# Differential attention's scores: one fp32 product or three fp32r products of split queries and keys

## The chip, the cores and the metric

The kernel runs on one core of one Trainium2 chip. The metric is the time of one execution on the device in microseconds. Three runs of the kernel before gave 3485.47, 3486.98 and 3488.18 us, median 3486.98.

## What is computed

Two stacks of two layers each run over 1024 tokens of width 1024, all in float32. The first stack mixes convolutions, a windowed attention and a neighbourhood attention. The second one has, per layer, a chunkwise retention, a differential attention, an output product and a gated feed-forward part. The change is in the differential attention of the second stack:

```
def diff_attention(q, k, v, lam):        # q, k: (B, S, 4 heads, 2 maps, 64)   v: (B, S, 4, 128)
    for i in range(S // 128):            # 8 blocks of 128 queries
        q0, kend = 128 * i, 128 * (i + 1)
        s = einsum('bqhjd,bkhjd->bhjqk', q[:, q0:kend], k[:, :kend]) * d ** -0.5
        s = s - slopes * dist            # ALiBi
        s = where(dist >= 0, s, -inf)    # causal
        p = softmax(s)
        a = p[:, :, 0] - lam * p[:, :, 1]
        outs.append(einsum('bhqk,bkhe->bqhe', a, v[:, :kend]))
```

Each head has two maps (j = 0, 1) whose softmaxes are subtracted, so a block of queries has 4 heads x 2 maps of scores against all keys up to its own block.

## The kernel before, in words

Everything is kept transposed: a chunk is 128 channels on the partitions by 1024 tokens. `st` is a store of 23 such slots in SBUF. Dense products are done to fp32 accuracy with three fp32r matmuls: every operand is split into a rounded part (`hi`) and the rest (`lo`), and hi·hi, hi·lo and lo·hi are summed in PSUM. A dense product (line 784) of 128 output channels uses two PSUM banks (0 and 1, or 2 and 3), is evacuated by VectorE (DVE), and counts in the semaphores `done` (TensorE) and `taken` (DVE). GpSimd (POOL) splits the weights for the next products (lines 619 and 622, in the values' stage 646 and 649) when `done` frees their buffer.

The differential attention of a layer is a list of 40 steps on each of three engines, written out by hand. Unit u = 4n + t is head t of query block n (n from 0 to 7), 32 units in all. The keys of a block are up to 8 tiles of 128; blocks 0 to 3 are one piece of 128, 256, 384 or 512 columns, blocks 4 to 7 are two pieces (384 and 256, 384 and 384, 512 and 384, 512 and 512). For a piece there is a pair of scores, one for each map: map j lies on the partitions 64j to 64j + 63 of the head's slot (queries in slots 4 to 7, keys in 18 to 21), so the two matmuls of a pair use different rows of the array, and write banks 4 and 5.

Step u of **TensorE** does in this order: turn the first group of tiles of unit u - 3 (line 926, bank 6); the scores of unit u's first piece (line 876); in some steps turn back a block's heads (line 960); weigh the values with unit u - 4 (line 943, bank 7); turn the second group; the scores of the second piece. Between the steps it does the matmuls of five dense products of the output projection (26 to 30), spread by the cuts (0, 7, 14, 20, 34, 40): a `product` first waits for `taken` of the one before.

Step u of **VectorE**: the mix of the two maps of unit u - 2 (lines 1842, 1843, 1847); the bias and running minimum of the first piece, once for each map (line 1825, `CUSTOM_DVE_ANT_0`, then a short read of its accumulator), which reads banks 4 and 5 and signals `biased`; the same for the second piece; and in steps with u % 4 of 0 and 1 the root and the factor of a block's heads (lines 1740 to 1745, 1853, 1860, 1874). At each cut it adds a dense product to x (line 1683).

Step u of **ScalarE** (ACT): it copies the turned groups out of bank 6 (line 1320), does the two exponentials of unit u - 1 (line 1306), and in steps with u % 4 of 3 copies the weighed block out of bank 7 and squares it (lines 1331, 1335); at the end of a block it writes the turned-back heads into slots 4 to 7 (line 1346).

The order of a pair before: the matmul of map 0 waits for `biased` of the previous map 0, the one of map 1 for `biased` of the previous map 1.

Just ahead of the attention TensorE runs the last value product (line 818) and the dense products 24 and 25. ScalarE issues the load of the bias table after value product 22; VectorE evacuates those values (line 1675), adds product 24 to x, waits for the table, adds product 25 to x and starts. Product 26 waits until product 24 has been added.

The two attentions of the first stack, windowed (`gqa`) and neighbourhood (`na`), already score with three fp32r products (line 897), with the parts made by `key_hi`, `query_hi` (ScalarE) and `key_lo`, `query_lo` (VectorE, lines 1784 to 1794).

## Time and profile before

| | |
|---|---|
| median of three runs | 3486.98 us (3485.47 to 3488.18) |
| the profiled execution | 3486.82 us, of which the span is 3484.7 us |
| TensorE busy | 3402.9 us, 98% |
| VectorE busy | 1954.8 us, 56% |
| ScalarE busy | 977.4 us, 28% |
| GpSimd busy | 1485.9 us, 43% |
| chain that ended last | TensorE 82%, issue 9%, VectorE 6%, GpSimd 2% |
| of it lines 784 and 1201 (dense products) | 44% and 23% |
| lines 943 and 926 (attention's values and turns) | 3% and 2% |
| old scores, line 876 | 384 records, 1392.0 to 2713.1 us |

The differential attentions lie at about 1392 to 1560 us and, in the second layer, at about 2580 to 2750 us. A busy TensorE isn't TensorE at its peak: matmuls overlap, and a record's duration holds its latency. In rows with "x4" four records follow each other closely and the duration is from the first start to the last end. A row's bracket gives the engine's idle time before it and what ended that. The granted clock (PEclk) is 1.00 at 2.4 GHz and 0.50 at 1.2 GHz.

### The profile page before, as it was taken

What the parts mean: (1) busy time and instruction counts of PE and PEld (TensorE: products, weight loads), DVE (VectorE), ACT (ScalarE), POOL (GpSimd) and SP (SyncE); (2) the same over time, 40 slices, a digit from 0 to 9 for tenths busy, and PEclk for the clock granted to TensorE, in tenths of its full rate; (3) what the DMA queues carried; (4) which work ended last, traced back from release to release, by engine and by line L of the source; (5) the groups of instructions that cost most, each with busy time, mean ns of one, the idle gap of its engine ahead of it and who ended that gap; (6) DMA issues with size and microseconds to landing.
All of it is one profiled execution on the core that took longest, in us unless ns stands there. A gap on an engine that the chain in (4) does not pass through costs nothing.

```text
span 3484.7 us, 43637 instructions
## 1 busy us (share of the span) xinstructions
PE 3402.9 (98%) x17144; PEld 2785.2 (80%) x17144; DVE 1954.8 (56%) x2937; ACT 977.4 (28%) x1831; POOL 1485.9 (43%) x952
## 2 busy tenths in 40 slices
PE   8999999999999999999999999999998999999997
PEld 7888788888788989567888888889885778888885
DVE  5777645777647143768656542332457775655315
ACT  2220442230342000655333320100035543333102
POOL 4435324435324433016555535643330365564543
PEclk9999999999999999999999999999999999999998
DMA  4112102102101111003222152111110122223411
GB/s 152 43 41 67 57 25 85 43 31 83 58 19 43 50 43 66 13 13 121 85 79 85 73 205 84 54 50 54 37 55 7 67 97 79 85 79 133 154 69 73
DMA packets 72821, 240.38 MB, mean 69 GB/s; under 512 B 21952, under 2 KB 22336, under 8 KB 66240
## 3 DMA queue, kind: packets, MB, share of 16 engines
q1 hardware_dynamic: 50112, 205.54, 16.6%
q10 hardware_dynamic: 22528, 32.31, 2.9%
q8 instruction: 127, 2.08, 0.2%
q14 instruction: 54, 0.44, 0.0%
HBM read 196.94 MB, written 41.68 MB: 68 GB/s over the span
## 4 chain that ended last, share of the span: by engine, by line
PE 82%; issue 9%; DVE 6%; POOL 2%; DMA 1%; ACT 1%; ACTq 0%; DVEq 0%; POOLq 0%
PE ps L784 44%; PE ps L1201 23%; PE ps L818 5%; PE ps L943 3%; PE ps L897 2%; PE ps L926 2%; POOL w_lo L622 1%; DVE st L1983 1%; POOL w_hi L619 1%; DVE st L1701 1%; DVE in_lo L1692 0%; DVE sl_r L2343 0%; PE ps L833 0%; PE ps L1121 0%; DVE xt L1683 0%
## 5 line engine op out<-in xcount | busy, mean ns | idle before, releaser
L619 POOL TENSOR_TENSOR w_hi<-w_raw,ones_r 128x512 fp32r<-128x512 f32 x316 | 406.5, 1286 | 1402.3 <-PE ps L784 1372.8
L1201 PE MATMUL ps<-sl_r,sl_r 128*128 128x512 f32 x3696 | 845.7, 391 | 5.1 <-DVE sl_r L2293 2.9
L1201 PEld LDWEIGHTS ps<-sl_r,sl_r 128*128 128x128 f32 x3696 | 696.1, 189 | 153.2 <-DVE sl_r L2293 3.8
L784 PE MATMUL ps<-in_hi,w_hi 128*128 128x512 f32 x1920 | 613.4, 401 | 14.8 <-DVE in_lo L1692 10.3
L784 PE MATMUL ps<-in_hi,w_lo 128*128 128x512 f32 x1920 | 600.8, 394 | 0.0
L784 PE MATMUL ps<-in_lo,w_hi 128*128 128x512 f32 x1920 | 598.9, 393 | 0.0
L622 POOL TENSOR_TENSOR w_lo<-w_raw,w_hi 128x512 fp32r<-128x512 f32 x316 | 465.4, 1473 | 24.8
L784 PEld LDWEIGHTS ps<-in_hi,w_hi 128*128 128x128 f32 x1920 | 348.4, 189 | 106.4 <-issue 38.7
L784 PEld LDWEIGHTS ps<-in_hi,w_lo 128*128 128x128 f32 x1920 | 358.4, 189 | 81.3 <-issue 5.7
L784 PEld LDWEIGHTS ps<-in_lo,w_hi 128*128 128x128 f32 x1920 | 359.7, 189 | 79.6 <-issue 4.4
L784 PE MATMUL ps<-sl_r,w_hi 128*128 128x512 f32 x1408 | 376.5, 389 | 0.2
L706 POOL TENSOR_TENSOR sl_r<-sl,sl_r 128x1024 fp32r<-128x1024 f32 x88 | 221.9, 2524 | 308.6 <-ACT sl_r L1557 303.4
L1683 DVE TENSOR_TENSOR xt<-xt,ps 128x1024 f32<-128x1024 f32 x112 | 136.7, 1220 | 351.4 <-PE ps L784 350.7
L2310 DVE TENSOR_TENSOR sl_r<-raw_pair,sl_r 128x1024 fp32r<-128x1024 f32 x84 | 196.9, 2383 | 216.5 <-ACT sl_r L1557 216.5
L784 PEld LDWEIGHTS ps<-sl_r,w_hi 128*128 128x128 f32 x1408 | 264.2, 188 | 55.9 <-DVE sl L2337 1.1
L1667 DVE TENSOR_TENSOR st<-ps,rfac 128x1024 f32<-128x1024 f32 x88 | 107.4, 1223 | 244.9 <-PE ps L784 227.0
L784 PE MATMUL ps<-sl_r,w_lo 128*128 128x512 f32 x704 | 216.7, 389 | 0.0
L1320 ACT ACTIVATE st<-ps 128x384 f32<-128x384 f32 (+3 forms) x256 | 122.9, 480 | 331.8 <-PE ps L926 331.3
L943 PEld LDWEIGHTS ps<-st 128*128 128x128 f32 x1504 | 184.3, 193 | 26.5 <-ACT st L1320 15.3
L1983 DVE SCALAR_TENSOR_TENSOR st<-st,cur 128x1023 f32<-128x1023 f32 (+14 forms) x128 | 199.5, 1559 | 2.0
L943 PE MATMUL ps<-st 128*128 128x64 f32 (+1 forms) x1504 | 198.0, 274 | 0.0
L1574 ACT ACTIVATE ps<-ps 128x512 f32<-128x512 f32 x132 | 76.8, 582 | 296.3 <-PE ps L1201 296.3
(218 smaller groups left out, 4249.2 us busy)
## 6 DMA issues: line engine op xcount, KB each, us to landing
w_raw<-w_in SPq DMA_DIRECT2D x184, 512.0 KB, 3.2
raw_pair<-w_ffn SPq DMA_DIRECT2D x44, 1024.0 KB, 4.8
hid_kept<-sl SPq DMA_DIRECT2D x44, 512.0 KB, 2.6
sl<-hid_kept SPq DMA_DIRECT2D x44, 512.0 KB, 8.5
x_put_away<-xt SPq DMA_DIRECT2D x16, 512.0 KB, 7.7
xt<-x_put_away SPq DMA_DIRECT2D x16, 512.0 KB, 6.2
xt<-x_in ACTq DMA_DIRECT2D x8, 512.0 KB, 8.0
space_lo<-c_alibi ACTq DMA_DIRECT2D x2, 2048.0 KB, 8.7
```

The lines of the kernel that those rows point to most:

```text
L619: pool.tensor_tensor(w_hi[:, j, cols], w_raw[:, j, cols], ones[:, 0:1].broadcast_to([P, HALF]), ALU.mult).then_inc(pool_own, 1)
L622: rest = pool.tensor_tensor(w_lo[:, j, cols], w_raw[:, j, cols], w_hi[:, j, cols].bitcast(F32), ALU.subtract)
L706: pool.tensor_tensor(sl_r[:, RING[p % 2][lo], :], pair_sums(p)[i], sl_r[:, RING[p % 2][hi], :].bitcast(F32), ALU.subtract).then_inc(pair_s ...
L784: last = pe.matmul(ps[:, 2 * j + h, :], w[:, w_slot, (w_k + k) * P:(w_k + k + 1) * P], part[:, k0 + k, h * HALF:(h + 1) * HALF], start=(k ...
L818: last = pe.matmul(out, x[:, k, tokens], w[:, 0:2, k * P:(k + 1) * P], start=(k == 0 and b % 2 == 0 and x is in_hi and w is w_hi), stop=(k ...
L943: last = pe.matmul(ps[:, 7, t * width:(t + 1) * width], turned_buffer(kind, g)[:, b * P:(b + 1) * P], value(t, kt), start=(kt == tiles[0]) ...
L1201: last = pe.matmul(ps[:, to[name], :], ring(sl_r, p, wp[w])[:, k * P:(k + 1) * P], half_of(sl_r, xp[x], k), start=(name in ("P1", "P5") an ...
L1320: act.activation(turned_buffer(kind, g)[:, 0:w], ps[:, 6, 0:w], ACT.Copy).then_inc(turned_out.handle, 1)
L1667: dve.tensor_tensor(to, ps[:, 2 * j:2 * j + 2, :].rearrange("p a b -> p (a b)"), rfac[:, :], ALU.mult).then_inc(taken.handle, 1)
L1683: last = dve.tensor_tensor(xt[:, c, :], xt[:, c, :], flat(ps, 2 * (n % 2), 2), ALU.add)
L1983: return dve.scalar_tensor_tensor(acc[:, a:b], source[:, a + d:b + d], weight, acc[:, a:b], ALU.mult, ALU.add)
L2310: dve.tensor_tensor(lo, source, hi.bitcast(F32), ALU.subtract).then_inc(pair_lo.handle, 1)
```

## The change

Queries and keys of the differential attention are split as in the other two attentions, and each score becomes three fp32r products. In detail:

- The four key slots (18 to 21) are copied, rounded, into slots 14, 16, 17 and 22 by ScalarE, and VectorE overwrites them with the rests. ScalarE does this after it has issued the table's load, VectorE after it has evacuated the values and before the first addition to x. The queries of blocks 0 and 1 follow on both.
- The rounded queries lie in a ring for two blocks in `rfac`; the rests overwrite the queries in slots 4 to 7. For blocks 2 to 7 ScalarE makes the rounded part at the end of step 4n - 3, VectorE the rest in step 4n - 2, after its second piece.
- `rfac` held the finished heads; these now share the buffer with the raw heads in slot 15. ScalarE's copy of raw heads waits for `back` in place of `headed` of two blocks earlier.
- TensorE waits for the query rest at a block's first unit. A pair of scores is six matmuls after one wait for `biased` of the previous pair's second map; each map's third product signals `scored`.

```
             if kind == "dif":                                  # head_buffer
-                return rfac[:, (n % 2) * HALF:(n % 2 + 1) * HALF]
+                return raw_buffer(n)

+        K_HI_DIF = (14, 16, 17, 22)
+            if kind == "dif":                                  # key_parts
+                return st[:, 18 + c, :], st_r[:, K_HI_DIF[c], :], st_r[:, 18 + c, :]
+            if kind == "dif":                                  # query_parts
+                block = slice(n * P, (n + 1) * P)
+                ring = rfac_r[:, :].rearrange("p (b t q) -> p b t q", b=2, t=4)
+                return st[:, 4:8, block], ring[:, n % 2], st_r[:, 4:8, block]

                     if kind == "dif":                          # TensorE, scores(u, i)
+                        if t == 0 and i == 0:
+                            pe.wait_ge(qk_lo.handle, qk_lo.at(stack, l, split_index(kind, n)))
+                        _, q_hi, q_lo = query_parts(kind, n)
+                        _, k_hi, k_lo = key_parts(kind, t)
                         for piece in pieces_of(tiles_of_round(kind, n))[i:i + 1]:
-                            for j in range(2):
-                                p, rows = state["p"], slice(HD * j, HD * (j + 1))
-                                if p >= 2:
-                                    pe.wait_ge(biased.handle, biased.at(stack, l, p0 + p - 1))
-                                pe.matmul(ps[:, 4 + j, 0:len(piece) * P], st[rows, 4 + t, n * P:(n + 1) * P],
-                                          st[rows, 18 + t, cols], start=True, stop=True).then_inc(scored.handle, 1)
-                                state["p"] += 1
+                            cols, p = slice(piece[0] * P, (piece[-1] + 1) * P), state["p"]
+                            if p >= 2:
+                                pe.wait_ge(biased.handle, biased.at(stack, l, p0 + p))
+                            for q, k in ((q_hi, k_hi), (q_lo, k_hi), (q_hi, k_lo)):
+                                for j in range(2):
+                                    rows = slice(HD * j, HD * (j + 1))
+                                    last = pe.matmul(ps[:, 4 + j, 0:len(piece) * P], q[rows, t, :], k[rows, cols],
+                                                     start=(q is q_hi and k is k_hi), stop=(k is k_lo))
+                                    if k is k_lo:
+                                        last.then_inc(scored.handle, 1)
+                            state["p"] += 2

-                        act.wait_ge(headed.handle, headed.at(stack, l, r0 + n - 1))
+                        act.wait_ge(back.handle, back.at(stack, l, r0 + n - 1))
-                    if kind != "dif" and u % 4 == 1 and 2 <= u // 4 + 1 < NB:
+                    if u % 4 == 1 and 2 <= u // 4 + 1 < NB:
                         query_hi(stack, l, kind, u // 4 + 1, p0)
+                for c in range(4):                             # ScalarE, ahead of the attention
+                    key_hi(1, l, "dif", c)
+                query_hi(1, l, "dif", 0)
+                query_hi(1, l, "dif", 1)

-                    if kind != "dif" and u % 4 == 2 and 2 <= u // 4 + 1 < NB:
+                    if u % 4 == 2 and 2 <= u // 4 + 1 < NB:
                         query_lo(stack, l, kind, u // 4 + 1)
                 evacuate_values(l, 22, 4, 10, 1)               # VectorE, ahead of the attention
+                for c in range(4):
+                    key_lo(1, l, "dif", c, c + 1)
+                for n in range(2):
+                    query_lo(1, l, "dif", n)
                 add_to_x(1, l, 24, 0)
```

## Rows read from the trace of the kernel before

**Rows 1.** Busy time in stretches: length, PE, PEld, DVE, ACT, POOL, granted clock, DMA
```profile
1392.00:1560.00 168.00, 154.19 (x821) 103.14 (x821) 124.96 (x412) 96.88 (x260) 17.75 (x16) 0.97 0.03 10
1433.00:1438.00 5.00, 4.64 (x15) 2.80 (x16) 3.88 (x12) 0.86 (x2) 0.00 (x0) 0.50 0.00 1
```

**Rows 2.** Groups of TensorE's instructions by shape, 1380 to 1610 us, the old scores
```profile
L876 PE MATMUL ps<-st 64*128 64x512 f32 x64 | 22.5, 672 | 0.6 <-DVE small L1825 0.4
L876 PE MATMUL ps<-st 64*128 64x384 f32 x80 | 21.8, 535 | 2.3 <-DVE small L1825 2.3
L876 PE MATMUL ps<-st 64*128 64x256 f32 x32 | 6.9, 428 | 0.7 <-DVE small L1825 0.7
L876 PE MATMUL ps<-st 64*128 64x128 f32 x16 | 2.3, 322 | 0.1
```

**Rows 3.** Timeline (start us, us, engine, line): old pairs issued together
```profile
1457.14 0.70 PE L876 MATMUL ps<-st 64*128 64x256 f32 x4
...
1500.61 0.92 PE L876 MATMUL ps<-st 64*128 64x384 f32 x4
...
1506.09 1.13 PE L876 MATMUL ps<-st 64*128 64x512 f32 x4
```

**Rows 4.** Timeline, block 7: units 30 and 31, VectorE and TensorE in turn
```profile
1517.94 0.68 DVE L1825 CUSTOM_DVE_ANT_0 st<-ps,space_lo 128x512 f32<-128x512 f32 x1
...
1518.69 1.73 PE L876 MATMUL ps<-st 64*128 64x512 f32 x4 [0.44 <-DVE small L1825]
...
1519.30 0.29 PEld L876 LDWEIGHTS ps<-st 64*128 64x128 f32 x2 [0.32 <-DVE small L1825]
1520.03 0.75 DVE L1825 CUSTOM_DVE_ANT_0 st<-ps,space_lo,small 128x512 f32<-128x512 f32 x1 [0.79 <-PE ps L876]
...
1520.71 0.75 DVE L1825 CUSTOM_DVE_ANT_0 st<-ps,space_lo,small 128x512 f32<-128x512 f32 x1
...
1520.94 1.70 PE L876 MATMUL ps<-st 64*128 64x512 f32 x4
```

**Rows 5.** Timeline, block 6: a second piece and the next first piece
```profile
1494.74 1.52 PE L876 MATMUL ps<-st 64*128 64x384 f32 x4 [0.53 <-DVE small L1825]
...
1497.29 1.13 PE L876 MATMUL ps<-st 64*128 64x512 f32 x4
```

**Rows 6.** Waits, 1392 to 1560 us: us in total, times, longest
```profile
PEld ps L876 <- DVE small L1825: 12.0, 37, 1.1
```

**Rows 7.** Timeline, neighbourhood attention: pairs of three fp32r products, and their reader
```profile
934.36 0.96 PE L897 MATMUL ps<-st_r 64*128 64x512 f32 x6
...
935.54 0.69 DVE L1825 CUSTOM_DVE_ANT_0 space_hi<-ps,st 128x512 f32<-128x512 f32 x1 [4.03 <-PE ps L897]
...
939.87 0.79 PE L897 MATMUL ps<-st_r 64*128 64x384 f32 x6
...
943.24 0.62 PE L897 MATMUL ps<-st_r 64*128 64x256 f32 x6
```

**Rows 8.** Groups of VectorE's instructions by shape, 1392 to 1570 us (busy us, mean ns)
```profile
L1874 DVE TENSOR_TENSOR rfac<-st,small 128x512 f32<-128x512 f32 x8 | 5.5, 692 | 0.3
L1695 DVE TENSOR_TENSOR in_lo<-st,in_hi 128x1024 fp32r<-128x1024 f32 x4 | 4.6, 1220 | 0.2 <-issue 0.2
```

**Rows 9.** Timeline ahead of the attention: VectorE, GpSimd and ScalarE
```profile
1370.91 7.69 DVE L1695 TENSOR_TENSOR in_lo<-st,in_hi 128x1024 fp32r<-128x1024 f32 x4 [10.39 <-ACT in_hi L1236]
...
1381.20 2.36 DVE L1675 TENSOR_TENSOR st<-ps,small 128x1024 f32<-128x1024 f32 x2 [2.61 <-PE ps L818]
...
1384.83 1.29 POOL L649 TENSOR_TENSOR w_lo<-w_raw,w_hi 128x512 fp32r<-128x512 f32 x1
...
1392.18 1.22 DVE L1683 TENSOR_TENSOR xt<-xt,ps 128x1024 f32<-128x1024 f32 x1 [4.29 <-PE ps L784]
...
1393.64 0.40 ACT L1306 ACTIVATE space_hi<-space_hi,small 128x128 f32<-128x128 f32 x1 [20.00 <-DVE small L1825]
```

**Rows 10.** Timeline, the stall in unit 15's step
```profile
1433.36 1.11 PE L926 MATMUL ps<-ident,space_hi 128*128 128x128 f32 x4 [4.42 <-DVE space_hi L1847]
```

More of the change, by code:

```diff
@@ L266, in build @@
         st = sb("st", [P, SLOTS, S])
+        base_rfac = top[0]
         rfac = sb("rfac", [P, S])
@@ L281, in build @@
         st_r = sb("st_r", [P, SLOTS, S], F32R, at=base_st)
+        rfac_r = sb("rfac_r", [P, S], F32R, at=base_rfac)
         xt_r = sb("xt_r", [P, KC, S], F32R, at=base_xt)
@@ L379, in build @@
         bias_ready = signal("bias_ready", 1)
-        qk_hi = signal("qk_hi", 1 + NB + 2 + NB)
-        qk_lo = signal("qk_lo", 1 + NB + 2 + NB)
+        qk_hi = signal("qk_hi", 1 + NB + 2 + NB, 4 + NB)
+        qk_lo = signal("qk_lo", 1 + NB + 2 + NB, 4 + NB)
         x_put = signal("x_put", 16)
@@ L480, in split_index @@
         def split_index(kind, n):
-            return {"gqa": 1, "na": 1 + NB + 2}[kind] + n + 1
+            return {"gqa": 1, "na": 1 + NB + 2, "dif": 4}[kind] + n + 1
         def rv(n, t):
@@ L868, in scores @@
                     if kind == "dif":
+                        if t == 0 and i == 0:
+                            pe.wait_ge(qk_lo.handle, qk_lo.at(stack, l, split_index(kind, n)))
+                        _, q_hi, q_lo = query_parts(kind, n)
+                        _, k_hi, k_lo = key_parts(kind, t)
                         for piece in pieces_of(tiles_of_round(kind, n))[i:i + 1]:
-                            cols = slice(piece[0] * P, (piece[-1] + 1) * P)
-                            for j in range(2):
-                                p, rows = state["p"], slice(HD * j, HD * (j + 1))
-                                if p >= 2:
-                                    pe.wait_ge(biased.handle, biased.at(stack, l, p0 + p - 1))
-                                pe.matmul(ps[:, 4 + j, 0:len(piece) * P], st[rows, 4 + t, n * P:(n + 1) * P],
-                                          st[rows, 18 + t, cols], start=True, stop=True).then_inc(scored.handle, 1)
-                                state["p"] += 1
+                            cols, p = slice(piece[0] * P, (piece[-1] + 1) * P), state["p"]
[9 more added lines that the diff above has]
+                            state["p"] += 2
                         return
```

## The prediction, made before the result was known

> **What bounds the kernel now.** I read the page first: TensorE is nearly always busy and the chain that ended last lies mostly on it, so whatever makes TensorE's queue longer or shorter moves the end. Then I asked for the stage of the change alone. A layer of the second stack has one such stage, and the two layers run alike to a few hundredths of a microsecond, so I work one (1392 to 1560 us) and count it twice. There TensorE is busy 154.2 of 168 us, VectorE 125.0, ScalarE 96.9 [rows 1]. So TensorE has only 14 us of idle time, but VectorE is at 74% and the two hand work back and forth. Per layer the old scores are 48 pairs (j = 0 and 1, the two halves of the partitions). An fp32 matmul is two records, so a pair is four: 16 pairs of 512 columns, 20 of 384, 8 of 256, 4 of 128 [rows 2]. In time order the pairs come in two sorts: issued together they take 0.70, 0.92 and 1.13 us for 256, 384 and 512 columns [rows 3]; where j = 1 waits for VectorE by itself, 1.5 to 1.7 us [rows 4, 5]. The list of waits has the weight loads of the old scores stopped by VectorE's bias-and-minimum instruction (L1825) 37 times for 12.0 us [rows 6].
>
> **The change part by part.** *Fewer passes on TensorE.* The neighbourhood attention already scores with the same three fp32r products, six matmuls on 64 rows, at L897: 0.62, 0.79 and 0.96 us for 256, 384 and 512 columns [rows 7]. Against the fp32 pairs issued together that is 0.08, 0.13 and 0.17 us less, so at most 8 x 0.08 + 20 x 0.13 + 16 x 0.17 = 6.0 us per layer on TensorE. For 128 columns no fp32r row exists. Bounds: nothing saved or lost, up to each of the three products as dear as a whole fp32 pair, 2 x 0.5 us more for each of 4 pairs (0.5 us is my estimate, less than the 0.70 of 256 columns), 4 us per layer. I take nothing, since the three products above cost less than one fp32 pair at every width shown; the upper end stays in the range.
>
> *A wait moved.* Before, the matmul of j = 0 waited only for the bias of the previous j = 0, the one of j = 1 for the previous j = 1. After it both wait for the previous j = 1. Queued behind that wait on TensorE are all six matmuls, and then the weighing, the turns and the filler products. Follow it in block 7 [rows 4]. VectorE starts the first piece's j = 0 at 1517.94, TensorE starts the second piece at 1518.69 as soon as that is done, its j = 1 is released at 1519.30, and VectorE starts the second piece at 1520.03 (it waited 0.79). After the change nothing starts before 1519.30, and from a start to VectorE's first use of the bank L897 takes 935.54 - 934.36 = 1.18 us [rows 7]: 1520.48, so 0.45 us later. The fp32 matmul took 1.34 from start to use, 1520.03 - 1518.69. The second piece's passes are cheaper, yet the cycle VectorE - TensorE - VectorE gets longer, for it now holds VectorE's second instruction too (0.7, as the 0.68 of [rows 4]). With 384 columns the same working gives 0.36, and 0.41 and 0.49 for the mixed widths of blocks 4 and 6. In blocks 4 to 7 there are 15 cycles from one second piece to the next; 9 of them end in a pair that waited so (1.17 to 1.73 us long, as the 1.52 of [rows 5]): 9 x 0.42 = **3.8 us lost**.
>
> *The other six cycles* are paced by TensorE itself, or by the turns that share its queue. Block 7 again [rows 4]: from the second piece's start to the end of the next first piece was 1520.94 + 1.70 - 1518.69 = 3.95 us, with both pairs split. After it, VectorE starts 1.18 after the start, needs 0.68 + 0.75 for its two instructions, TensorE starts 0.07 later and takes 0.96: 3.64, and less the overlap of VectorE's two tail reads (0.08 each) about 3.5, so 0.45 us less. In block 6 the same stretch was 1497.29 + 1.13 - 1494.74 = 3.68 [rows 5] and would be about 3.1, but VectorE then has the new query rest to do in that cycle and I leave 0.28. Taking 0.4 for the three without a query rest and 0.3 for the three with one: **2.1 us gained**.
>
> *Query parts.* Six times per layer inside the attention VectorE gets a subtraction of 128x512 (0.69 [rows 8]) and ScalarE a copy. ScalarE waits for TensorE in these steps and hides its copy; if that cover went it would cost six copies at no more than the 0.69 of the same size on VectorE, 4 us. Of VectorE's six, three stand in the cycles just counted. Of the other three I count one (0.6 us, block 2's, where the chain of waits of this layer runs on VectorE); behind the others it waits for TensorE anyway.
>
> *Ahead of the attention.* Four key subtractions of 128x1024 (1.22 each) and two of queries (0.69 each) [rows 8], 6.3 us, go in on VectorE behind the values and ahead of the first addition to x. VectorE idled 4.29 us ahead of the second addition [rows 9], and ScalarE had been idle 20.00 us [rows 9], so its six copies are hidden: each ends before VectorE asks for it. The 6.3 us start behind the values, which ended at 1381.20 + 2.36 = 1383.6 [rows 9], so they and the first addition (1.2) end at about 1391.1, 1 us before TensorE wants the bank at 1392.1. But GpSimd is splitting weights there: two of its instructions are still to come, the later at 1384.83 [rows 9]. Four subtractions of this shape with three of GpSimd's beside them took 7.69 us [rows 9] against 4.6 without [rows 8], 1.0 us for each of GpSimd's. So VectorE ends 2 us later, 1 too late: **1.0 us lost**. GpSimd's own delay is covered: its half is wanted at 1392. The Trainium skill (SBUF — State Buffer, "SBUF: two separate sides") says that a VectorE instruction with two SBUF inputs and a GpSimd one that reads SBUF exclude each other for the whole instruction. By that rule the trace agrees in kind, and at 1.29 us apiece this term would be up to 1.6.
>
> *Blocks 0 to 3* have one piece per unit. Their pairs save 4 x 0.08 + 4 x 0.13 + 4 x 0.17 = 1.5 us on TensorE, of which I count half, since VectorE paces some of them; it also paces the 4.42 us stall at 1433 [rows 10], which stays. Behind this stall the granted clock is 0.50, the lower level (1.2 GHz) [rows 1]: one pair runs there with its passes twice as long, which saves 0.4 more. *At the end* the last pair saves 0.2 on the way to the last head. The raw heads now share their buffer with the finished ones and ScalarE waits for a turn-back four steps older: nothing, and if it came late ScalarE would hold TensorE's bank 7. Nothing of the change lies on SP's or GpSimd's queue.
>
> **Sum per layer:** 1.0 + 0.6 - 0.8 - 0.4 + 3.8 - 2.1 - 0.2 = +1.9 us; twice +3.8. The profiled execution took 3486.8 us (span 3484.7 and 2.1 around it), so 3490.6; the median of the runs shown is 0.2 above it: **3490.8 us**. That is +0.1%. About 0.2% (7 us) is what a measurement of this kernel can tell from no change. So I forecast no telling difference, on the slow side.
>
> **The rivals.** *TensorE's passes count (faster).* If TensorE is what ends last everywhere, the full 6.0 us per layer come off and nothing is added: 3486.8 - 11.9 + 0.2 = 3475 us. For it: 154 of 168 us busy. Against it: the 37 waits, and VectorE's waits for a score of 0.79 us where it has nothing else to do. Chance 0.19.
>
> *VectorE paces every cycle (slower).* The place is blocks 4 to 7. There VectorE would be the last at each second piece, so the six gaining cycles gain nothing (+2.1) and all six query rests come on top (6 x 0.69 less the 0.6 already counted, +3.5), with the last 0.2 lost too: 1.9 + 5.8 = 7.7 per layer, 3486.8 + 15.4 + 0.2 = 3502 us. It decides from where VectorE's work in a cycle, with the wait of 1.18 in it, exceeds TensorE's; by my working the six cycles lie within 0.5 us of that point. For it: VectorE at 74% before it gets 4 us more in this stage. Against: two of the six cycles have 0.4 us to spare. Chance 0.25.
>
> *The products are not what they seem.* Six loads and six matmuls in place of four records could be paid per instruction, as for the 128 columns above: 4 us per layer, 3499 us. Rows 7 speak against it from 256 columns on. Chance 0.05.
>
> **How the numbers follow.** The forecast has 0.51, its own range is 3484 to 3498; a part of it (0.03) lies above 3494. Faster by over 0.2%: 0.19. Slower by over 0.2%: 0.25 + 0.05 + 0.03 = 0.33. Within: 0.48. The range goes from 3478 (short of the faster rival, of which about half is left out) to 3503.
>
> **What would show it.** TensorE: six records a pair at about 0.62, 0.79 and 0.96 us, none split any more, and more idle time ahead of them released by L1825; the busy time of the stage down by several us while the stage is longer. VectorE: a wait of 1.0 to 1.2 us ahead of every second piece. At 1392 us: a gap of about 1 us on TensorE that ends with the addition to x. The second piece of block 7's third unit starting 0.4 later after its predecessor than before. It is wrong if the weight loads' waits for L1825 don't grow, if the stage is shorter by 3 us or more, or if the last product of the stage moves by another amount than the end of the kernel.

## The result, and the profile after

The changed kernel takes **3493.66 us** in the median (3490.50 to 3500.85, 12 runs), the kernel before 3487.28 in the same session (3485.47 to 3491.22, 12 runs): ratio 1.0018, 95% interval 1.0010 to 1.0025. It is slower by 6.4 us; the forecast was 3490.8. That is just under the 7 us that the forecast called telling, but the interval leaves out 1: with twelve runs of each kernel the difference is clear of noise.

The profiled execution of the kernel after was the longest of its twelve, 3500.85 us. Its page:

```profile
span 3499.0 us, 44085 instructions
...
PE 3386.1 (97%) x17336; PEld 2799.0 (80%) x17336; DVE 1978.5 (57%) x2961; ACT 994.1 (28%) x1855; POOL 1483.8 (42%) x952
```

TensorE is busy for 16.8 us less than before (3402.9), and the span is 14.3 us longer. Of these 14.3 us, 4.7 were there before the first differential attention began (its dense product 24 starts at 1385.71, before at 1381.00), in code that the change leaves alone; in the profiles of the runs below, the same code brings that product to anywhere from 1380.7 to 1386.0. Two stages hold 9.3 us. I measure a stage from product 24's first matmul to the last turn-back of heads: 166.59 us in both layers before, 169.96 and 172.56 after. The rest is 0.5 between the stages and -0.3 behind the second.

The busy time from the first scores to the last turn-back, first in the kernel before, then in the one after (columns as in [rows 1]), the groups of the new scores by shape, and the list of waits:

```profile
1392.00:1547.60 155.60, 141.79 (x772) 92.87 (x771) 117.80 (x405) 92.28 (x255) 13.76 (x12) 0.98 0.03 11
1397.50:1555.70 158.20, 130.15 (x867) 96.70 (x867) 120.64 (x411) 95.51 (x261) 13.19 (x12) 0.97 0.03 11
```
```profile
L890 PE MATMUL ps<-st_r,rfac_r 64*128 64x384 f32 x80 | 16.1, 397 | 7.6 <-DVE small L1845 7.5
L890 PE MATMUL ps<-st_r,rfac_r 64*128 64x512 f32 x64 | 14.9, 459 | 6.4 <-DVE small L1845 6.3
...
L890 PE MATMUL ps<-st_r,rfac_r 64*128 64x256 f32 x32 | 5.0, 328 | 2.8 <-DVE small L1845 2.7
```
```profile
PEld ps L890 <- DVE small L1845: 22.8, 29, 1.7
PE ps L890 <- DVE small L1845: 16.5, 23, 1.4
```

L890 are the scores now, L1845 is the bias and minimum (before: L876, L1825). The weight loads' wait for VectorE has grown from 12.0 us in 37 places [rows 6] to 22.8 in 29, and the matmuls idle 7.5, 6.3 and 2.7 us where the old ones idled 2.3, 0.4 and 0.7 [rows 2]. TensorE was busy 141.8 of 155.6 us and is now busy 130.2 of 158.2. So the passes did get cheaper, and what they freed became idle time behind the joined wait. Block 7, to be held against [rows 4]:

```profile
1526.34 0.69 DVE L1845 CUSTOM_DVE_ANT_0 st<-ps,space_lo 128x512 f32<-128x512 f32 x1
...
1527.09 0.50 PE L890 MATMUL ps<-st_r,rfac_r 64*128 64x512 f32 x2 [1.22 <-DVE small L1845]
1527.43 0.39 PE L890 MATMUL ps<-st_r 64*128 64x512 f32 x2
1527.66 0.40 PE L890 MATMUL ps<-st_r,rfac_r 64*128 64x512 f32 x2
1527.99 0.66 PE L942 MATMUL ps<-ident,space_hi 128*128 128x128 f32 x4
1528.28 0.75 DVE L1845 CUSTOM_DVE_ANT_0 st<-ps,space_lo,small 128x512 f32<-128x512 f32 x1 [1.24 <-PE ps L890]
...
1529.76 0.50 PE L890 MATMUL ps<-st_r,rfac_r 64*128 64x512 f32 x2 [1.11 <-DVE small L1845]
```

Read it from the top. VectorE starts its second instruction. TensorE has been idle for 1.22 us and starts only when that one is done. Its six matmuls take 0.90 us (1527.09 to 1527.99). VectorE starts 1.19 us after the first of them, having waited 1.24. In this cycle the two engines never work on scores at the same time: it holds one full turn of VectorE (two instructions) and one of TensorE (six matmuls).

The forecast left out something that these windows of the kernel after show. The first two lines are the same code in layer 1 and layer 2, and so are the next two; the last is layer 2 ahead of its last turn-back:

```profile
1421.00:1426.00 5.00, 4.50 (x31) 3.23 (x31) 4.01 (x16) 2.99 (x8) 0.00 (x0) 1.00 0.01 3
2613.00:2618.00 5.00, 4.58 (x22) 3.58 (x22) 3.29 (x13) 2.48 (x7) 0.00 (x0) 0.66 0.01 2
...
1481.00:1486.00 5.00, 4.87 (x29) 4.03 (x29) 2.95 (x10) 2.67 (x7) 0.00 (x0) 0.68 0.00 0
...
2673.00:2678.00 5.00, 4.42 (x36) 3.32 (x35) 4.04 (x12) 2.03 (x5) 0.00 (x0) 1.00 0.00 0
...
2730.00:2736.00 6.00, 4.17 (x23) 3.70 (x23) 4.31 (x18) 3.48 (x7) 0.00 (x0) 0.79 0.00 0
```

The column after the five engines is the granted clock. Before, it fell inside the attention at one place per layer, behind the 4.42 us stall [rows 1, 10]. Now it falls to the lower level (0.50, 1.2 GHz) at further places, and not at the same ones in both layers. What ran ahead of such a place, in either layer:

```profile
1421.10 0.55 PE L942 MATMUL ps<-ident,space_hi 128*128 128x128 f32 x3 [1.07 <-DVE space_hi L1867]
1422.05 0.44 PE L890 MATMUL ps<-st_r,rfac_r 64*128 64x384 f32 x2 [0.41 <-DVE small L1845]
...
1425.05 0.50 PE L890 MATMUL ps<-st_r,rfac_r 64*128 64x512 f32 x2
```
```profile
2612.84 0.55 PE L942 MATMUL ps<-ident,space_hi 128*128 128x128 f32 x3 [1.07 <-DVE space_hi L1867]
2613.80 0.49 PE L890 MATMUL ps<-st_r,rfac_r 64*128 64x384 f32 x2 [0.42 <-DVE small L1845]
...
2618.38 0.50 PE L890 MATMUL ps<-st_r,rfac_r 64*128 64x512 f32 x2
```

Idle times of 1.07 and 0.41 us in both, yet from one pair to the next it is 3.00 us in layer 1 and 4.58 in layer 2: this fall cost 1.58 us on the spot. About 0.4 of it was made good by 2621 us, where layer 2 is 1.2 us behind its twin.

### The profile page after: what moved, and what is told of

Read it like the earlier page. It is cut to its first block, busy times and chain, and to the rows that moved or that the text cites. A ratio compares the mean times of both kernels' runs of the same rounds, so it can differ in the third digit from the quotient of the medians.

```text
span 3499.0 us, 44085 instructions
## 1 busy us (share of the span) xinstructions
PE 3386.1 (97%) x17336; PEld 2799.0 (80%) x17336; DVE 1978.5 (57%) x2961; ACT 994.1 (28%) x1855; POOL 1483.8 (42%) x952
## 4 chain that ended last, share of the span: by engine, by line
PE 81%; issue 9%; DVE 7%; POOL 2%; DMA 1%; ACT 1%; ACTq 0%; DVEq 0%; POOLq 0%
PE ps L793 44%; PE ps L1217 23%; PE ps L827 5%; PE ps L959 3%; PE ps L913 2%; PE ps L942 1%; POOL w_lo L631 1%; DVE st L2003 1%; POOL w_hi L628 1%; DVE st L1721 1%; PE ps L842 1%; DVE in_lo L1712 0%; DVE sl_r L2367 0%; DVE xt L1703 0%; PE ps L1137 0%
## 5 line engine op out<-in xcount | busy, mean ns | idle before, releaser
L793 PE MATMUL ps<-in_hi,w_hi 128*128 128x512 f32 x1920 | 615.6, 402 | 14.9 <-DVE in_lo L1712 10.4
L793 PE MATMUL ps<-in_hi,w_lo 128*128 128x512 f32 x1920 | 601.3, 394 | 0.0
L793 PE MATMUL ps<-in_lo,w_hi 128*128 128x512 f32 x1920 | 599.8, 394 | 0.0
L793 PEld LDWEIGHTS ps<-in_hi,w_hi 128*128 128x128 f32 x1920 | 349.6, 190 | 103.9 <-issue 35.5
L793 PEld LDWEIGHTS ps<-in_lo,w_hi 128*128 128x128 f32 x1920 | 360.6, 189 | 77.7 <-issue 1.7
L793 PEld LDWEIGHTS ps<-in_hi,w_lo 128*128 128x128 f32 x1920 | 358.6, 189 | 78.6 <-issue 2.5
L793 PE MATMUL ps<-sl_r,w_hi 128*128 128x512 f32 x1408 | 376.5, 389 | 0.2
L793 PEld LDWEIGHTS ps<-sl_r,w_hi 128*128 128x128 f32 x1408 | 264.1, 188 | 55.9 <-DVE sl L2361 1.1
L793 PE MATMUL ps<-sl_r,w_lo 128*128 128x512 f32 x704 | 216.6, 389 | 0.0
L959 PEld LDWEIGHTS ps<-st 128*128 128x128 f32 x1504 | 186.7, 195 | 12.5 <-issue 7.6
```

The costliest lines, as they stand in the source:

```text
L793: last = pe.matmul(ps[:, 2 * j + h, :], w[:, w_slot, (w_k + k) * P:(w_k + k + 1) * P], part[:, k0 + k, h * HALF:(h + 1) * HALF], start=(k ...
L959: last = pe.matmul(ps[:, 7, t * width:(t + 1) * width], turned_buffer(kind, g)[:, b * P:(b + 1) * P], value(t, kt), start=(kt == tiles[0]) ...
```

## The experiments

The twelve kernels of the experiments were timed in three sessions, each beside the kernel before (its medians were 3487.89, 3487.75 and 3488.20 us). Medians are of 11 executions, of 8 for apart_joined and of 5 for fill and one_own. Each interval against the kernel before is some 6 us wide (9 to 10 for those of 5), so two kernels whose medians lie within about 3 us of each other can't be told apart. "First to last" is the stretch from the first to the last pair of scores, for layer 1 and layer 2 of the profiled execution.

| kernel | median us | against before (95%) | first to last, us |
|---|---|---|---|
| before | 3487.28 | | 133.16, 133.16 |
| changed | 3493.66 | 1.0018 (1.0010 to 1.0025) | 135.75, 136.73 |
| joined_fp32 | 3493.19 | 1.0017 (1.0008 to 1.0026) | 137.8, 137.8 |
| maps_apart | 3481.15 | 0.9978 (0.9969 to 0.9987) | 129.7, 130.3 |
| first_early | 3486.87 | 1.0005 (0.9996 to 1.0014) | 132.27, 132.28 |
| apart_joined | 3495.20 | 1.0025 (1.0014 to 1.0035) | 138.50, 136.19 |
| fill | 3501.13 | 1.0039 (1.0025 to 1.0053) | 139.39, 139.44 |
| one_product | 3480.30 | 0.9982 (0.9973 to 0.9991) | 131.21, 131.22 |
| one_own | 3475.49 | 0.9964 (0.9950 to 0.9977) | 125.04, 130.62 |
| no_rests | 3491.85 | 1.0011 (1.0002 to 1.0020) | 133.9, 138.2 |
| query1_later | 3493.92 | 1.0016 (1.0007 to 1.0025) | 137.4, 137.7 |
| rest_between | 3493.86 | 1.0019 (1.0010 to 1.0028) | 136.48, 136.39 |
| no_start_rests | 3493.87 | 1.0016 (1.0007 to 1.0025) | 136.66, 136.53 |
| best2 | 3479.95 | 0.9977 (0.9968 to 0.9986) | 130.58, 130.72 |

### The wait alone, in the kernel before

```
-                            for j in range(2):
-                                p, rows = state["p"], slice(HD * j, HD * (j + 1))
-                                if p >= 2:
-                                    pe.wait_ge(biased.handle, biased.at(stack, l, p0 + p - 1))
+                            if state["p"] >= 2:
+                                pe.wait_ge(biased.handle, biased.at(stack, l, p0 + state["p"]))
+                            for j in range(2):
+                                p, rows = state["p"], slice(HD * j, HD * (j + 1))
```

> The kernel before, with one edit: the fp32 pair of scores starts only when the previous pair's second map has been biased, as in the changed kernel. No split, no new work on VectorE or ScalarE, same four records a pair. Theory (the joined wait lengthens the cycle VectorE - TensorE - VectorE): in the nine cycles of blocks 4 to 7 that VectorE paces each gets longer by its second instruction, 0.5 to 0.6 us, so about +5 us per layer and +8 to +12 us in all, 3495 to 3499 us; no pair of 512 columns is longer than 1.15 us any more. Rival (TensorE has other work to fill the wait; the loss of the changed kernel is VectorE's new work): within 2 us of the kernel before.

3493.19 us: 5.3 over the kernel before in its session. The wait alone costs nearly as much as the whole change; that it was free is refuted, though the range of the theory (3495 to 3499) was missed by 2 us. Its waits, from the list for the stage (L875 scores, L1824 bias):

```profile
PEld ps L875 <- DVE small L1824: 22.8, 31, 1.5
...
PE ps L875 <- DVE small L1824: 14.7, 22, 1.3
```

They are the changed kernel's waits, with the old fp32 matmuls behind them. Each layer's stage is 4.6 us longer (first to last 137.8 for 133.2), as the theory said, and the granted clock has no further falls inside it: one stretch at the lower level per layer, behind the stall. That the two stages' 9.2 us end as 5.3 is in good part the clock behind them. The 6 us behind the last turn-back of layer 1, in the kernel before and in joined_fp32:

```profile
1547.60:1553.60 6.00, 6.00 (x22) 4.96 (x23) 4.00 (x4) 4.59 (x5) 0.00 (x0) 0.72 0.01 4
```
```profile
1552.20:1558.20 6.00, 6.00 (x29) 5.02 (x30) 4.34 (x4) 4.60 (x5) 0.00 (x0) 1.00 0.02 4
```

The granted clock is 0.72 there in the kernel before and 1.00 here, which gives 1.6 us back, and the same again in layer 2. In the changed kernel's profile it is 0.72 in both layers, as before.

### The three products with the old kind of wait

```
-                            if p >= 2:
-                                pe.wait_ge(biased.handle, biased.at(stack, l, p0 + p))
-                            for q, k in ((q_hi, k_hi), (q_lo, k_hi), (q_hi, k_lo)):
-                                for j in range(2):
+                            for j in range(2):
+                                if p >= 2:
+                                    pe.wait_ge(biased.handle, biased.at(stack, l, p0 + p - 1 + j))
+                                for q, k in ((q_hi, k_hi), (q_lo, k_hi), (q_hi, k_lo)):
```

> The changed kernel with the three products of map 0 issued first behind the wait for the previous map 0 alone, then the three of map 1 behind theirs, in all 48 pairs of a layer. The waits are those of the kernel before, but six matmuls on one half of the rows after the other no longer run two at a time: a pair of 512 columns takes 6 x 0.21 + 0.3 = 1.5 to 1.6 us where it took 0.96. Theory: the nine cycles paced by VectorE lose 0.5 us each (-4.5 per layer), the six paced by TensorE and the steps of blocks 0 to 3 gain up to 0.6 per pair (+5 to +9 per layer); in all 0 to +9 us against the changed kernel, 3494 to 3502 us, and which of the two it is shows per unit. Rival (only the waits count, the pairs' length is hidden): 8 to 10 us faster than the changed kernel.

**3481.15 us**, 6.7 below the kernel before and 12.5 below the changed one, with every product in place. I had priced a pair that is issued map by map at 1.5 us and was wrong. Two pairs of 512 columns (L887 scores), the first with map 1 released late, the second with both maps free:

```profile
1511.09 0.50 PE L887 MATMUL ps<-st_r,rfac_r 64*128 64x512 f32 x1
...
1511.43 0.39 PE L887 MATMUL ps<-st_r 64*128 64x512 f32 x1
...
1511.66 0.49 PE L887 MATMUL ps<-st_r,rfac_r 64*128 64x512 f32 x2
...
1512.00 0.39 PE L887 MATMUL ps<-st_r 64*128 64x512 f32 x1
...
1512.23 0.39 PE L887 MATMUL ps<-st_r,rfac_r 64*128 64x512 f32 x1
...
1512.56 1.83 PE L968 MATMUL ps<-st 128*128 128x128 f32 x14
```
```profile
1527.51 0.50 PE L887 MATMUL ps<-st_r,rfac_r 64*128 64x512 f32 x2
1527.85 0.40 PE L887 MATMUL ps<-st_r 64*128 64x512 f32 x2
1528.08 0.40 PE L887 MATMUL ps<-st_r,rfac_r 64*128 64x512 f32 x2
1528.41 0.74 PE L793 MATMUL ps<-in_hi,w_hi 128*128 128x512 f32 x2
```

The counts tell: x1, x1, x2, x1, x1 is one map after the other, 1.47 us. x2, x2, x2 is both maps side by side, 0.90 us, as in the changed kernel, although map 1's matmuls stand three places later in the queue. So the order costs nothing where both maps are free, and where map 1 is late, map 0 is done early. The weight loads' wait for VectorE is back to 9.3 us in 22 places. The stages take 163.96 and 164.46 us, 4.8 less than before together. Another 1.7 came off between the stages and 2.5 behind the second, of which 1.6 each time directly behind the last turn-back. The stretch from the first of these turn-backs on, of the kernel before and of maps_apart (L960 and L985 are the turn-backs, L784 and L793 the dense products):

```profile
1547.59 0.96 PE L960 MATMUL ps<-ident,rfac 128*128 128x128 f32 x4 [2.04 <-DVE rfac L1874]
1548.20 1.20 PE L784 MATMUL ps<-in_hi,w_lo 128*128 128x512 f32 x2
```
```profile
1549.95 0.66 PE L985 MATMUL ps<-ident,st 128*128 128x128 f32 x4 [2.02 <-DVE st L1903]
1550.36 0.70 PE L793 MATMUL ps<-in_hi,w_lo 128*128 128x512 f32 x2
```

The same two matmuls take 1.20 us and 0.70: behind nearly the same idle time the clock fell in one kernel (granted 0.72 over the next 6 us) and not in the other (1.00). So of the 9.0 us that the profile gains from product 24 on, 4.8 lie in the stages and 3.2 in two falls of the clock that don't come.

### Order and wait taken apart

first_early keeps the products in turn but lets map 0's first one go when map 0 is free:

```
-                            if p >= 2:
-                                pe.wait_ge(biased.handle, biased.at(stack, l, p0 + p))
                             for q, k in ((q_hi, k_hi), (q_lo, k_hi), (q_hi, k_lo)):
                                 for j in range(2):
                                     rows = slice(HD * j, HD * (j + 1))
+                                    if p >= 2 and q is q_hi and k is k_hi:
+                                        pe.wait_ge(biased.handle, biased.at(stack, l, p0 + p - 1 + j))
```

> The six products of a pair stay in the changed kernel's order (both maps in turn), but the wait is split: the first product of map 0 waits for map 0's bias alone, the first of map 1 for map 1's. No work is left out. It asks what made the maps apart 12.5 us faster than the changed kernel. Theory A (it is that map 0's scores are complete 0.5 us or more before map 1's, so that VectorE can begin its bias): here map 0 can't be complete before the second and third product behind map 1's, only one of its matmuls goes early, so 3490 to 3494, at most 3 us of gain. Theory B (it is TensorE's waiting: any product that it can begin while map 1's bias runs is time gained, and keeps the clock up): most of the 12.5 us come back, 3482 to 3487.

apart_joined is maps_apart's order behind the one joined wait.

> The products are issued map by map, as in maps_apart, but all behind the one joined wait of the changed kernel. No work is left out. It completes the square of order and wait: in turn and joined 3493.66 (the changed kernel), in turn with map 0's first product early 3486.87, map by map with own waits 3481.15. Theory (the wait is all; with both maps released together the two row halves run side by side in either order, as in the pair of 0.90 us at 1527.51 in the trace of maps_apart): 3492 to 3495. Rival (the order gives a share of its own, since map 0's scores are then ready for VectorE before map 1's; or it costs, if the halves run after one another, 1.47 for 0.90 us): 3487 to 3490, or over 3500.

first_early came out at 3486.87, the upper end of theory B's range and half way between the two kernels: by the medians 6.8 of the 12.5 us come with one early matmul, the other 5.7 only when map 0's whole score is finished early. The split is rough, for its runs lie apart: seven at 3485.0 to 3487.0 with a granted clock of 0.992, four at 3490.4 to 3494.5 with 0.989 or 0.990. In its profile, of the first sort, the stages take 166.5 us each, as in the kernel before. apart_joined, 3495.20, is no better than the changed kernel: the order by itself gives nothing. It is the wait.

### Is it the work done early, or TensorE kept active?

```
                             if p >= 2:
+                                pe.wait_ge(biased.handle, biased.at(stack, l, p0 + p - 1))
+                                for _ in range(2):
+                                    pe.matmul(ps[:, 4, 0:len(piece) * P], q_hi[0:HD, t, :], k_hi[0:HD, cols],
+                                              start=True, stop=True)
                                 pe.wait_ge(biased.handle, biased.at(stack, l, p0 + p))
```

> The changed kernel's joined wait for all six products, but behind map 0's own wait two extra matmuls of map 0's first product are issued, whose result is written over. No work is left out; it adds TensorE activity where the engine would wait and moves no needed work ahead. It tells the two halves of first_early's gain (6.8 us) apart. Theory A (what counts is needed work done before map 1's bias is ready): no gain, and where both maps are ready the extra pair costs 0.4 us: 3494 to 3501. Theory B (what counts is TensorE idling, by which the granted clock falls to its lower level at more places, as at 2613.8 and 1480 of the changed kernel's trace): the granted clock rises to 0.992 or more and the time falls to 3488 to 3492.

3501.13 us, 7.5 over the changed kernel. Both layers (columns as in [rows 1]):

```profile
1392.40:1531.90 139.50, 129.09 (x834) 95.47 (x834) 109.65 (x372) 83.32 (x230) 8.72 (x8) 0.98 0.03 9
2587.60:2727.10 139.50, 129.07 (x834) 95.45 (x834) 109.59 (x372) 83.35 (x230) 8.67 (x8) 0.98 0.02 9
```

TensorE is busier, the further falls of the clock are gone (the stretch that took 3.00 and 4.58 us takes 3.0 in both layers), and the granted clock of the profiled run is 0.992, as theory B said. But the time went theory A's way: the extra matmuls cost more than the clock gave. The run doesn't price the two by themselves, since every pair carries the extra work, also where both maps are free. It shows that such activity doesn't pay here; needed work done early does.

### TensorE's passes

one_product leaves one product of each score, behind the joined wait; one_own the same with a wait for each map.

> Only the product of the two rounded parts is left of each score in the differential attention (no rest of a query or key enters; the rests are still computed): 2 matmuls a pair instead of 6, one wait on map 1 as in the changed kernel. It prices TensorE's two further passes in the cycle. The pairs fall from 0.90, 0.71 and 0.55 us (512, 384 and 256 columns) to about 0.47, 0.36 and 0.25 by the first two records of a pair, some 0.4 us for each of the 126 or so pairs of both layers that are in a cycle. Theory (in most cycles the pair lies on the path, between map 1's bias and the next map 0's bias, with VectorE idle): 0.4 us x 2 pairs x 31 units x 2 layers = 50 us if all of it lay there; VectorE was busy 106.2 of 132 us of this stretch, so not more than 26 us a layer can go, and the tail and the turns hold some of it: a gain of 15 to 40 us, 3454 to 3479. Rival (the cycle is set by VectorE's own work and the wait alone; the pair's length is hidden behind the projection's matmuls that stand between): 3488 to 3494, no gain.

> Only the product of the two rounded parts is left of each score (the rests are computed and not used), and each map's matmul waits for its own bias. Beside one_product (the same with one joined wait, 3480.3 us) it gives the price of the joined wait where TensorE's passes are few, and beside maps_apart (3481.15) the price of the two further passes where the waits are apart. Theory (the joined wait costs what the bias of map 1 takes beyond map 0's, 0.3 to 0.5 us in the nine cycles that VectorE sets, whatever the passes): first scores to last score 131.2 us with the joined wait, 127 to 129 us here, 3472 to 3477. Rival (with one pass VectorE is the floor, and maps_apart's 141.5 and best2's 130.6 us are already on it): 3478 to 3481, no gain over one_product.

With the joined wait, two thirds of the scores' passes are worth 13.4 us (3480.30), just short of the 15 to 40 that I expected and about what maps_apart gets with all passes in place. Separate waits take another 4.8 us off (3475.49). So a joined wait costs 5.3 us with fp32 pairs, 12.5 with three products, 4.8 with one. That is not "the second bias instruction, whatever the passes", as I wrote. I read it as more work for map 0 to do early where there are three products. No run tests that reading, and these totals hold changes of the clock too (the 5.3 us are 9.2 in the stages). (The 141.5 us of maps_apart in the second expectation are counted from product 24; its first to last is 129.7.)

one_own also holds the cleanest measurement of the clock, the same code twice in one execution:

```profile
1396.00:1521.10 125.10, 104.18 (x554) 72.77 (x554) 109.18 (x372) 83.53 (x230) 8.67 (x8) 0.96 0.03 9
2576.10:2706.80 130.70, 111.51 (x554) 79.01 (x554) 109.45 (x372) 84.04 (x231) 8.68 (x8) 0.89 0.03 9
```

VectorE and ScalarE are busy for the same time; TensorE's granted clock is 0.96 in one and 0.89 in the other, and the second takes 5.6 us more.

### The rests on VectorE

no_rests leaves out the six query rests inside the attention; rest_between puts them between the two pieces' scores; query1_later moves the second query block's rest behind the first addition to x; no_start_rests leaves out the six subtractions ahead of the attention.

```
-                    if u % 4 == 2 and 2 <= u // 4 + 1 < NB:          # VectorE, no_rests
+                    if kind != "dif" and u % 4 == 2 and 2 <= u // 4 + 1 < NB:

+                    if kind == "dif" and u % 4 == 2 and 2 <= u // 4 + 1 < NB:   # rest_between
+                        query_lo(stack, l, kind, u // 4 + 1)
                     if u < len(units) and kind == "dif":
                         scores(u, 1)

-                for n in range(2):                                    # query1_later
-                    query_lo(1, l, "dif", n)
+                query_lo(1, l, "dif", 0)
                 add_to_x(1, l, 24, 0)
+                query_lo(1, l, "dif", 1)

-                for c in range(4):                                    # no_start_rests
-                    key_lo(1, l, "dif", c, c + 1)
-                for n in range(2):
-                    query_lo(1, l, "dif", n)
```

> The changed kernel without the six subtractions of query rests inside the attention; for blocks 2 to 7 the second product takes the rounded queries again, so the scores of these blocks lack the rest's term and have hi x hi twice. TensorE's work is the same. Theory: of the six per layer one in the first blocks (0.6 us) and parts of the three in blocks 4 to 6 are on the path: 1 to 2 us per layer, 2 to 4 us faster than the changed kernel, 3490 to 3492 us. Rival (VectorE paces every cycle): all six count, 8 us faster, 3485 us.

> One edit on the changed kernel: the subtraction that makes the rest of query blocks 2 to 7 stands between the two pieces' scores of its unit on VectorE instead of after them. No work is left out. The run without these six rests came out 1.8 us under the changed kernel, so this is what the place can give at most. Theory: between the pieces the subtraction (0.69 us) runs while VectorE would have waited for the second pair; the cycle gets shorter by up to 0.3 us in twelve places but the second pair's bias comes later where TensorE was early: 3490 to 3494. Rival (the place is as bad as any other where VectorE sets the cycle): 3495 to 3500, each of the twelve costing 0.2 to 0.5 us more.

> The changed kernel with VectorE's subtraction for the queries of block 1 moved behind the first addition to x. Same work. Theory: the 0.7 us gap on TensorE ahead of the first scores, which ends with this addition, closes in both layers: 1.0 to 1.4 us faster, 3492 us. Rival (the gap is made good later, as VectorE paces what follows): no change, the first scores 0.7 us earlier but the end of the stage where it was.

> The changed kernel without the subtractions ahead of the attention: the keys' rests and those of query blocks 0 and 1 aren't computed, and the rounded parts are used in their place. It prices the forecast's 1.0 us a layer for the start. Theory (the six subtractions hold up VectorE's add to x and the first scores, 0.8 us of gap, in each of two layers, and what is won there stays won): 1.6 us less, 3491.5 to 3492.5. Rival A (the gap is given back at the next wait, as with query1_later, where the gap closed from 11.78 to 11.16 us and the time stayed): 3493 to 3494.5. Rival B (VectorE's six operations, 0.7 to 1.2 us each, lie on the path in blocks 0 to 2, where VectorE is behind): 3486 to 3490.

no_rests came out 1.8 us lower, of the 8.3 us that its twelve subtractions take: they are mostly hidden. That gain isn't clear of noise (its runs reach from 3486.4 to 3497.2), and the other three can't be told from the changed kernel either. query1_later closed the gap at the start (product 24 to the first scores 11.16 us for 11.78), but its seventh pair came 11.0 us after the first where the changed kernel's came 10.5: the moved subtraction was in VectorE's way there. no_start_rests has no gap at all (11.0 us, as before) and its seventh pair comes at 11.1: of the 0.8 us that the gap is shorter, 0.6 are given back by then, in the first two blocks. That VectorE is what these blocks wait for is my reading.

### The best of them

maps_apart with query1_later's and rest_between's places:

> Three edits together on the changed kernel: every map's three products issued on their own behind that map's own wait (as in maps_apart, 3481.15 us), the second query block's rest put behind the first add to x, and the rest of query blocks 2 to 7 put between the two pieces' scores of its unit instead of after them. No work is left out. Theory: the maps apart carry all of the gain there is (3481), the moved second rest gave nothing by itself (3493.92 against 3493.66), and the moved rests cost the six cycles that TensorE set about as much as they give. In numbers: 3481 within 2 us. Rival A: with the maps apart the cycles are shorter, VectorE's order counts for more, and each of the six rests per layer (0.69 us) that no longer stands ahead of the mix saves up to a third of itself: 12 x 0.2 = 2.4 us, and the start up to 1 us: 3477 to 3479. Rival B: the rest between the pieces delays the second piece's bias in the cycles that VectorE sets, 12 x 0.4 us: 3484 to 3487.

3479.95 us (3477.25 to 3482.42), 0.23% under the kernel before and 0.39% under the changed one. The margin over maps_apart, 1.2 us, lies within both kernels' spreads. It is the fastest with all of the scores' products in place.

## Why the prediction was right, and where it was not

The forecast was no telling difference on the slow side, 3490.8 us in 3478 to 3503; 3493.66 lies in it, 2.9 us above. The side was right. That such a difference couldn't be told was not: the interval of 1.0010 to 1.0025 tells it. The steps, in the profiled execution against the profile before:

| step, us per layer | forecast | layer 1 | layer 2 |
|---|---|---|---|
| start, and up to unit 16's second piece | +0.4 | +0.43 | +2.37 |
| the 15 cycles of blocks 4 to 7 | +1.7 | +2.94 | +1.97 |
| tail | -0.2 | 0.00 | +1.63 |
| sum | +1.9 | +3.37 | +5.97 |
| of it, falls of the clock at new or later places | 0 | 1.2 | 3.8 |
| sum without them | +1.9 | +2.2 | +2.2 |

The falls' shares come from setting each stretch against its twin in the other layer, so that the last row has to be nearly the same in both. In layer 1 it is 1.2, in a cycle near 1481 us that is 0.05 shorter than before in layer 2 (5.17 us). In layer 2 it is 2.2 up to unit 18 (1.58 at 2613.8, less 0.4 made good, and 0.9 where the clock came back later behind the stall), and 1.63 in the tail (24.06 for 22.43 us).

- **The joined wait** was the term that decided, and its mechanism held. In blocks 4 to 7, nine cycles were forecast to lose 3.8 us together; they lost 3.4 in layer 1 (0.17 to 0.49 each). From start to VectorE's first use it was 1.19 us for the 1.18 taken from [rows 7].
- **The other six cycles** were to gain 2.1 us. In layer 1 five of them gained 0.18 to 0.61, 1.6 together; the sixth lost 1.16 by a fall of the clock, for 0.05 gained in layer 2. The size was nearly right, the clock was missing.
- **The products** cost what the neighbourhood attention's did: from first start to last end 0.97 us for 512 columns (1527.09 to 1527.66 + 0.40) against 0.96 [rows 7]. For 128 columns, where no row existed, a pair took 0.48 us to the next matmul (1397.49 to 1397.97), where the old pair took 0.42 (1392.00 to 1392.42): next to nothing for four pairs, as assumed.
- **The start** was sized 1.0 and was 0.78. The chain is the one foretold, the key rests slowed beside GpSimd, then the addition to x:

```profile
1388.18 6.71 DVE L1808 TENSOR_TENSOR st_r<-st,st_r 128x1024 fp32r<-128x1024 f32 x4
...
1397.49 0.33 PE L890 MATMUL ps<-st_r,rfac_r 64*128 64x128 f32 x2 [0.71 <-DVE xt L1703]
```

  Four subtractions took 6.71 us where four without GpSimd took 4.6 [rows 8]: 2.1 us more beside two of GpSimd's instructions, and the forecast had 2. The Trainium skill (SBUF — State Buffer, "SBUF: two separate sides") has the two engines exclude each other for whole instructions. The trace agrees in kind, and its 2.1 us is a little below what that rule would make: an estimate of 2.3, from 1.04 and 1.29 us for these two instructions in the kernel before. What the forecast missed is that most of this 0.8 us is given back within two blocks; the time without it (no_start_rests, 3493.87) can't be told from the time with it.
- **Query rests inside** were charged 0.6 us a layer beyond what stood in the cycles; without all six the kernel was 0.9 a layer lower, which isn't clear of noise.
- **The clock is the term that was left at nothing.** The sum went by full-clock durations outside the old stall. "More idle time" on TensorE was foretold as a sign, but not that the granted clock would fall at more places. In the twelve timed runs of the changed kernel the mean granted clock and the time go together: 3491.3 us where it was 0.992 (2 runs), 3493.5 at 0.991 (6), 3496.9 at 0.989 (3), 3500.8 at 0.988 (1). Runs of the kernel before in the later sessions average 3487.2 us at 0.992 (32 runs) and 3488.2 at 0.991 (41), so at the same granted clock the changed kernel is 4.1 to 5.2 us slower, near the 3.8 of the forecast. It is a rough comparison: two kernels, and a mean over the whole execution with three digits. That the rest of the 2.9 us between forecast and median are these falls is what this order and the table suggest; only for the profiled execution was it traced place by place. The Trainium skill (TensorE: Matmul & The Clock Gate, "Part 1: The HAM clock gate") says that activity releases the throttle and its lack brings it back. The runs agree in kind: fill added activity and lost the falls (0.98 in both stretches above, 0.96 in the changed kernel from the first scores to the last). That doesn't settle where a given idle time brings a fall.

Of the rivals, that TensorE's passes count in full (3475) was wrong as put, since the freed passes became waits. But with each map's own wait 6.7 of these 11.9 us are there (3481), though some 3 of them are the clock behind the stages. That VectorE paces every cycle (3502) was wrong too: the six cycles that were to gain did gain, but for one with a fall of the clock, and leaving out the rests gave 1.8 us, not 7. That products are paid by the instruction was wrong at every width (0.06 us more for a pair of 128 columns, not 1).

None of the forecast's signs of being wrong came: the weight loads' waits grew, the stages got longer, and in the profile the last turn-back of heads came 14.6 us later for 14.3 at the end of the kernel. Of both, 4.7 were there before the first stage.

What stays open is what makes a given idle time cost a fall of the clock. No kernel tried here moves one such place and nothing else, so the clock's share of the 6.4 us is read from traces and not shown by an experiment. The joined wait's share is.

## What to carry to other kernels

When a fast path replaces one instruction by several, keep the waits where the old one had them: here a joined wait for two buffers that come free one after the other turned a gain of 6.7 us into a loss of 6.4. If two engines hand buffers back and forth, ask of each wait which half of the work could start without it, and issue that half whole. And where TensorE gets more idle time in a tightly coupled stage, add a term for its clock, with a spread as wide as one such fall (1.2 to 1.6 us here) for each new gap. Behind the stage look too: there a fall of 1.6 us that the old kernel had can be gone in the new one.

## What the runs showed of the hardware

- Matmuls on the two halves of the rows run side by side even when they are queued map by map, three after three: 0.90 us for a pair of six at 512 columns in maps_apart, the same as in turn. It took a wait between the maps to separate them (1.47 us).
- Whether the granted clock falls behind a short idle time isn't settled by that idle time: 1.07 and 0.41 us of it preceded both 3.00 us at full clock and 4.58 us with a fall, and 2.04 and 2.02 us behind the stage went either way too. A whole stage of the same code took 125.04 or 130.62 us by it, within one execution (one_own).
- A mean granted clock that is lower does not mean a slower kernel: one_own ran at 0.987 to 0.988 and was the fastest of all, fill at 0.990 to 0.993 and the slowest. It compares runs of one kernel only.
